# A mixer and expert block on one core: first adaLN pieces on TensorE in column strips, blocks 0 and 3 tile by tile, down chunks in column halves

## The reference

```python
u = modulate(rms_norm(x, norm_mix_g), sh_a, sc_a)      # h * (1 + scale) + shift
x = x + gt_a * mixer(u, w_in, ...)                     # mLSTM and dilated attention on one projection
u = modulate(rms_norm(x, norm_ffn_g), sh_f, sc_f)
x = x + gt_f * moe(u, router_w, ...)                   # 16 experts, group-limited top-2
return rms_norm(x, final_norm_g)
```

## Time and profile before

| | us |
|---|---|
| median of 3 runs | 624.14 |
| lowest, highest | 622.63, 625.4 |
| the profiled execution, whole | 625.4 |
| its span, first to last instruction | 623.5 |
| TensorE busy in the span | 579.7 (93%) |
| VectorE, ScalarE, GpSimd busy | 316.7, 229.3, 5.7 |

### The profile page before, as it was taken

One profiled execution on the slowest core, in us unless ns is written; L12 is line 12 of the kernel. 1 busy time (PEld: TensorE's weight loads), 2 busy tenths in 40 slices (PEclk: granted clock), 3 DMA queues, 4 the chain that ended last, 5 costly groups with the idle time before them and its releaser, 6 DMA issues.

```text
span 623.5 us, 8315 instructions
## 1 busy us (share of the span) xinstructions
PE 579.7 (93%) x3522; PEld 428.6 (69%) x3522; DVE 316.7 (51%) x467; ACT 229.3 (37%) x312; POOL 5.7 (1%) x14
## 2 busy tenths in 40 slices
PE   1599999999999999999999999989999999999784
PEld 0499988999998888999999885534543533533232
DVE  3797976767569786786464754312202122220203
ACT  4425748444555365376543434201201111110103
POOL 3000000000000000000000000000000000000000
PEclk9799999999999999999999998999999999999997
DMA  8996553785857944744599897399999999999981
GB/s 316 362 387 227 203 203 130 276 290 219 300 216 284 399 155 162 270 139 165 174 387 357 320 383 268 114 398 389 399 387 400 387 402 387 402 387 401 387 350 69
DMA packets 80584, 184.77 MB, mean 296 GB/s; under 512 B 5561, under 2 KB 5665, under 8 KB 78497
## 3 DMA queue, kind: packets, MB, share of 16 engines
q1 hardware_dynamic: 78018, 184.06, 79.6%
q10 hardware_dynamic: 2528, 0.16, 0.3%
HBM read 183.16 MB, written 1.05 MB: 295 GB/s over the span
## 4 chain that ended last, share of the span: by engine, by line
PE 82%; DMA 9%; DVE 4%; ACT 2%; SPq 2%; issue 1%; DVEq 0%; ACTq 0%
PE ps L1357 29%; PE ps L1365 15%; PE ps L1568 15%; PE ps L1580 7%; DMA ring<-in_w_down_e_dram 3%; DMA ring<-in_w_gate_e_dram 2%; DMA ring<-in_w_up_e_dram 2%; DMA raw<-in_w_in_dram 2%; PE ps L1604 2%; PE ps L1556 2%; PE ps L1345 1%; SPq L444 1%; PE ps L1523 1%; PE ps L1434 1%; PE ps L1470 1%
## 5 line engine op out<-in xcount | busy, mean ns | idle before, releaser
L803 DVE TENSOR_TENSOR lo<-raw,hi 128x2048 fp32r<-128x2048 f32 x52 | 118.8, 2291 | 43.3 <-ACT hi L539 43.0
L1357 PE MATMUL ps<-u_hi,hi 128*128 128x256 f32 x432 | 124.4, 288 | 1.1 <-DVE u_lo L869 1.1
L1357 PE MATMUL ps<-u_lo,hi 128*128 128x256 f32 x432 | 122.2, 283 | 0.0
L1357 PE MATMUL ps<-u_hi,lo 128*128 128x256 f32 x432 | 122.2, 283 | 0.0
L1568 PE MATMUL ps<-ring,xe_t 128*64 128x512 f32 x512 | 113.8, 594 | 7.6 <-DMA ring<-in_w_up_e_dram 3.9
L539 ACT CAST hi<-raw 128x2048 fp32r<-128x2048 f32 x52 | 98.7, 1906 | 51.4 <-PE ps L1357 24.6
L1568 PEld LDWEIGHTS ps<-ring,xe_t 128*64 128x64 f32 x512 | 37.5, 137 | 75.3 <-issue 75.2
L1357 PEld LDWEIGHTS ps<-u_hi,hi 128*128 128x128 f32 x432 | 82.8, 192 | 1.5 <-DVE u_lo L869 1.3
L1357 PEld LDWEIGHTS ps<-u_lo,hi 128*128 128x128 f32 x432 | 82.8, 192 | 0.2
L1357 PEld LDWEIGHTS ps<-u_hi,lo 128*128 128x128 f32 x432 | 82.8, 192 | 0.0
L1580 PE MATMUL ps<-ring,he_t 128*64 128x512 f32 x256 | 57.1, 596 | 1.5 <-DMA ring<-in_w_down_e_dram 0.7
(11 more groups left out here) (297 smaller groups left out, 803.3 us busy)
## 6 DMA issues: line engine op xcount, KB each, us to landing
raw<-in_w_in_dram SPq DMA_DIRECT2D x42, 1024.0 KB, 5.0
ring<-in_w_gate_e_dram SPq DMA_DIRECT2D x32, 1024.0 KB, 14.6
ring<-in_w_up_e_dram SPq DMA_DIRECT2D x32, 1024.0 KB, 14.2
ring<-in_w_down_e_dram SPq DMA_DIRECT2D x32, 1024.0 KB, 14.4
raw<-in_ada_w_dram SPq DMA_DIRECT2D x16, 1024.0 KB, 5.0
first_ada<-in_ada_w_dram SPq DMA_DIRECT2D x16, 512.0 KB, 11.6
raw<-in_w_branch_m_dram SPq DMA_DIRECT2D x4, 1024.0 KB, 7.2
raw<-in_w_out_dram SPq DMA_DIRECT2D x4, 1024.0 KB, 6.3
```

What stands on the lines that cost most here:

```text
L803: V.tensor_tensor(lo[b % RING][:], src[:], hi[b % RING][:].bitcast(F32), ALU.subtract).then_inc(lo_ready, 1)
L1357: ins = mm(dst, w[:, k, cols], x[:, k0 + k, :], start=(first and c % 2 == 0 and k == 0 and n == 0), stop=(end and k == KB - 1 and n == 2), ...
```

## The change

- **adaLN pieces.** Pieces 0 to 3 and 7 are multiplied by c on TensorE: four calls a piece, each with c's column broadcast to 32 columns as weights, each into its own 32 partitions of a PSUM bank (`row_sums`). VectorE copies the four rows of sums (`rows_out`), and four matmuls with a 0/1 matrix `pick_m` add the strips and turn them into columns. VectorE still sums pieces 4, 5 and 6 (semaphore `acc_done`), and two matmuls with ones add that sum to the strips of piece 7.
- **Order.** The plain matmuls ahead of the transposes are gone; pieces 0 and 1 stand there. A matmul in piece 2 to 3 and four behind the columns write a bank that nobody reads. In `FIRST` block 2 comes before piece 5. Block 3's load waits for `acc_done` 2, since piece 5 lies in its buffer.
- **Blocks 0 and 3** are rounded, split and multiplied tile by tile; block 0 is loaded in four DMAs.
- **Small loads.** The four small DMAs of ScalarE are issued by GpSimd after `chan1`.
- **ScalarE** loads the root's table ahead of the squares, and ahead of the last rounding of y at the end.
- **Down of the last pair.** Its four chunks are regrouped by columns: two hold columns 0 to 511 of both experts, whole contraction; the others, loaded in halves, columns 512 to 1023. `gate_y` and the splitting run by half, and four matmuls that nobody reads follow the first half's scatter.
- **Last norm.** Squares go half 0 first; VectorE multiplies half 0 by the gain early and ScalarE scales it, VectorE does half 1.

```diff
-FIRST = ([("ada", a) for a in range(4)] + [("w", 0), ("w", 1), ("ada", 4), ("ada", 5), ("w", 2), ("ada", 6), ("ada", 7),
+FIRST = ([("ada", a) for a in range(4)] + [("w", 0), ("w", 1), ("ada", 4), ("w", 2), ("ada", 5), ("ada", 6), ("ada", 7),
...
             for kind, n in FIRST:
-                if kind == "w":
+                if kind == "w" and n == 0:
+                    for k in range(KB):
+                        sp.dma_start(raw[0][:, k:k + 1, :], block_source((kind, 0))[:, k:k + 1, :]
+                                     ).then_inc(first_w[k] if k < KB - 1 else raw_loaded[0], 16)
+                elif kind == "w":
+                    if n == EARLY:
+                        sp.wait_ge(acc_done, 2)
...
-            for n in range(RSLOTS, CHUNKS):
+            for n in range(RSLOTS, CHUNKS - 4):
...
+            for q in range(2):
+                for e in range(2):
+                    n = CHUNKS - 2 + e
+                    sp.wait_ge(chunk_used, n - RSLOTS + 1)
+                    load_columns(n % RSLOTS, e, 1, (q,), last_loaded[e] if q else ring_loaded[n % RSLOTS])
...
+            after(pool, "chan1")
+            pool.dma_start(w_if[:], A["w_in"][0].rearrange("(k p) n -> p k n", p=P)[:, :, IF_AT:IF_AT + IF_N]).then_inc(small_loaded, 16)
+            pool.dma_start(gate_b[:], A["mlstm_gate_b"][0:1, :].broadcast_to([P, IF_N])).then_inc(small_loaded, 16)
+            pool.dma_start(rw[:], A["router_w"].rearrange("(k p) n -> p k n", p=P)).then_inc(small_loaded, 16)
+            pool.dma_start(rb[:], A["router_b"].rearrange("(a n) -> a n", a=1).broadcast_to([P, NE])).then_inc(small_loaded, 16)
...
+            act.wait_ge(consts_ready, 2)
+            A_(st[:, 36:37], ident[:, 0:1], ACT.Sqrt)
...
-            split_hi(0)
             after(act, "x_t")
...
+            def split_first(j):
+
+                hi_tile(j, 0)
+                hi_tile(j, 1)
+                u_hi_tile(j, 0)
+                u_hi_tile(j, 1)
+                hi_tile(j, 2)
+                u_hi_tile(j, 2)
+                hi_tile(j, 3)
+                u_hi_tile(j, 3)
...
+            def last_norm():
+
+                for n in range(2 * TT):
+                    if n:
+                        act.wait_ge(squared, n)
+                    last_square(n % TT, n // TT)
+                    if n >= TT:
+                        t = n - TT
+                        act.wait_ge(last_var, t + 1)
+                        A_(st[:, 32 + t:33 + t], st[:, 20 + t:21 + t], ACT.Sqrt).then_inc(last_sqrt, 1)
+                for t in range(TT):
+                    act.wait_ge(last_rms, t + 1)
+                    A_(result[:, t, 0:NB], result[:, t, 0:NB], ACT.Copy, scale=st[:, 34 + t:35 + t]).then_inc(out_act, 1)
...
+            def first_half(j, row_bank, col_bank):
+
+                rows_out(j, row_bank)
+                lo_tile(j, 0)
+                modulate(j, col_bank)
                 for k in range(KB):
-                    after(dve, f"u_hi0_{k}")
-                    event(V.tensor_tensor(u_lo[:, k, :], u_f32[:, k, :], u_hi[:, k, :].bitcast(F32), ALU.subtract), f"u_lo0_{k}")
...
+                    if k:
+                        lo_tile(j, k)
+                    u_tile(j, k)
...
+            first_half(0, 2, 3)
             split_lo(1)
             ada(4)
-            ada(5)
...
                 if s == 0:
+                    ada(5)
                     ada(6)
-                    ada(7)
-                    split_lo(EARLY)
-                    modulate(1, 7)
-                if s == 1:
-                    u_split_lo(1)
+                    first_half(1, 6, 7)
...
             for h in range(2):
+                dve.wait_ge(chunk_used, CHUNKS - 2 + 2 * h)
+                gate_y((h,))
                 dve.wait_ge(y_hi_ready, 2 * PAIRS - 1 + h)
                 split_y(h)
...
+            def row_sums(j, bank, a, start, stop):
+
+                pe.wait_ge(ada_landed[a], 32)
+                for i in range(2):
+                    for m in range(2):
+                        part, kk = 32 * (2 * i + m), 2 * (a % KB) + i
+                        ins = mm(ps[bank][part:part + 32, :], cs[:, kk:kk + 1].broadcast_to([P, 32]), first_ada[a][:, i, m, :],
+                                 start=start, stop=stop, skip_group_check=True)
+                ins.then_inc(rows_summed, 1)
+
             def mod_columns(j, bank):
 
-                pe.wait_ge(ada_done, 4 * (j + 1))
...
+                for c in range(KB):
+                    if c % 2 == 0:
+                        after(pe, f"row{j}_{c // 2}")
+                    ins = mm(ps[bank][:, 2 * c:2 * c + 2], ada_rows[:, j, c * P:(c + 1) * P], pick_m[:], start=True, stop=True,
+                             skip_group_check=True)
                 event(ins, f"mod_col{j}")
...
+            after(pe, "c_silu")
+            for a in range(2):
+                row_sums(0, 2, a, a == 0, False)
             after(pe, "x_norm")
-            for n in range(2):
-                mm(ps[2 + n][:], ident[:], x_in[:, 0, 0:NB], start=True, stop=True)
...
-            mod_columns(0, 1)
+            for a in (2, 3):
+                row_sums(0, 2, a, False, a == 3)
+                if a == 2:
+                    mm(ps[1][:], ident[:], first_ada[0][:, 0, 0, :], start=True, stop=True)
+            pe.wait_ge(pick_ready, 4)
+            mod_columns(0, 3)
+            for n in range(4):
+                mm(ps[1][:, 0:T], ident[:], first_ada[0][:, 0, 0, 0:T], start=True, stop=True)
...
-                        if s == EARLY - 1 and c == 2:
+                        if s == EARLY - 1 and c == 3:
                             after(pe, "x_up")
-                            mod_columns(1, 7)
+                            row_sums(1, 6, KT - 1, True, False)
+                            pe.wait_ge(acc_done, KB - 1)
+                            for m in range(2):
+                                ins = mm(ps[6][32 * m:32 * m + 32, :], ones[:, 0:32], acc_a[:, m, :], start=False, stop=True,
+                                         skip_group_check=True)
+                            ins.then_inc(rows_summed, 1)
...
+                            if s == EARLY - 1 and c == 3 and k == 2:
+                                mod_columns(1, 7)
...
+                    last_down(0, range(KB), group_slots(p * NPART + 4))
+                    slots = group_slots(p * NPART + 5)
+                    last_down(1, (0, 1), slots)
+                    for e in range(2):
+                        pe.wait_ge(last_loaded[e], 16)
+                    last_down(1, (2, 3), slots)
...
+                if h == 0:
+                    for _ in range(4):
+                        mm(ps[4][:], scat[1][:, 0:P], y_hi_e[:, 0:NB], start=True, stop=True)
```

More of the change, by code:

```diff
@@ L219, in build @@
         cs = small("cs", [P, KT])
+        pick_m = small("pick_m", [P, 2])
         st = small("st", [P, 40])
@@ L843, in _, with rows_out, lo_tile @@
             after(dve, "c_silu")
+            def rows_out(j, bank):
+                dve.wait_ge(rows_summed, (4, 6)[j])
+                for n in range(2):
+                    cols = slice(n * T, (n + 1) * T)
+                    event(V.tensor_copy(ada_rows[:, j, cols], ps[bank][:, cols]), f"row{j}_{n}")
+            def lo_tile(j, k):
+                b = EARLY * j
+                after(dve, f"hi{b}_{k}")
+                event(V.tensor_tensor(lo[b % RING][:, k, :], raw[POS[("w", b)] % RAW][:, k, :], hi[b % RING][:, k, :].bitcast(F32),
+                                      ALU.subtract), f"lo{b}_{k}")
             def modulate(j, bank):
@@ L1186, in fill_xe, with gate_y @@
                 ins.then_inc(xe_dve, 1)
-            def gate_y():
-                for h in range(2):
+            def gate_y(halves=(0, 1)):
+                for h in halves:
                     ins = V.tensor_tensor(y_e[:, h * NB:(h + 1) * NB], ps[6 + h][:], mod[:, 3, h * NB:(h + 1) * NB], ALU.mult)
@@ L1583, in down, with last_down @@
                                 ins.then_inc(chunk_used, 1)
+            def last_down(h, kk_of, slots):
+                for kk in kk_of:
+                    for s in range(2):
+                        w = ring[slots[s]][:].rearrange("p (k n) -> p k n", k=KB)
+                        ins = mm(ps[6 + h][64 * s:64 * s + 64, :], he_t[:, kk, s * SLOTS:(s + 1) * SLOTS], w[:, kk, :],
+                                 start=(kk == 0), stop=(kk == KB - 1))
+                        if kk == KB - 1:
+                            ins.then_inc(chunk_used, 1)
             def turn_slots(col, weights):
```

213 lines of the change are left out of this document (112 added, 101 removed).

## The result

The changed kernel took 618.0 us (median of ten runs, 617.07 to 621.85), the kernel before 624.31 beside it (ten runs, 622.52 to 626.61): ratio 0.9909, 95% interval 0.9884 to 0.9933.

A forecast was written before the change was run, and what follows sets the result against it. TensorE was taken to bound most of the span, with the expert stage bound by transfers whose start hangs on TensorE. Head 5.3 plus tail 1.9 made 7.2 us off the 624.1 median: 616.9 us, range 614.5 to 621.0.

The forecast's parts named there:

- Head, forecast 5.3: Start of the kernel up to block 4: block 4 starts at 50.75 instead of 56.0 us, 5.3 us earlier.
- Piece 1.05 and 1.9: adaLN pieces on TensorE: four strips side by side take 1.05 us a piece at full clock, 1.9 at half.
- Block 0 at 22.8 to 23.4: Start of block 0's matmuls: 22.8 to 23.4 us instead of 27.37.
- chan1 at 43.5, tile 0 at 44.4: Ahead of block 3: second scale and shift columns ready at 43.5 us, first tile of u at 44.4, starting block 3.
- 0.6 + 0.35 + 0.36 = 1.3 us: Within block 0: VectorE's time per tile, 1.3 us, below TensorE's 1.44, so TensorE leads if the clock stays up.
- Tail, forecast 1.9: End of the kernel, from the down halves to the last store: 1.9 us saved, with ends 0.8 and 3.
- the scatter's 0.43 us against 0.23: Last scatter on TensorE: each matmul takes 0.23 us instead of 0.43 if the clock stays up.
- A: Head: strips run only in pairs, head gain 2.4 us, total 619.8 us; chance 0.10.
- D: Head: strips run one after another, block 3 comes 5.8 us later, total 628.0 us; chance 0.05.
- B: Head: half clock lasts into block 0, which starts at about 25.5 us; head gain 2.5, total 619.7; chance 0.15.
- C: Before the experts: VectorE or a load swallows the head's gain, only the tail's stays, 622.2 us; chance 0.08.
- under 1 us for eight changes: Head: draining TensorE at eight changes of tiling mode costs under 1 us, and the sum stays.

The follow-up runs named there:

- both edits: The changed kernel without the filler matmul ahead of the fourth piece and with unused matmuls that hold the clock in the gaps: 616.66 us, ratio 0.9881.

## Why the prediction was right, point by point

**The size.** Forecast 7.2 us, medians 6.3, lower levels (617.83 against about 622.5) 4.7, profiled pair 8.6. That the medians agree with the sum is in part luck. Like with like, at the lower levels, the change is worth 4.7 us, 3.7 by the head and 1.0 by the end, against 5.3 and 1.9 forecast. The other 1.6 us come from the levels: the median run of the kernel before is one in which the clock had fallen more (624.3 against 622.5), that of the changed kernel is not. The forecast had no term for it. Nor had it one for the time outside the span: it took 1.9 us for both kernels, and the changed one has 0.3 more than the kernel before.

**Head, forecast 5.3, measured 4.7 by the profiled pair and 3.7 by the lower levels.** The mechanism stands, and in the profiled pair nearly every step. Piece 1.05 and 1.9: 1.06 and 1.93. Transposes end 17.2: 16.5. Third piece until 18.2: 17.5. Fourth until 20.1: 19.6. Columns 21.7: 21.24. Block 0 at 22.8 to 23.4: 22.98. split_lo(1) ends 29.2: 29.3. Issue of block 3's load 36.2: 36.22. The step that was mis-sized is "chan1 at 43.5, tile 0 at 44.4": chan1 was ready at 43.7, and the first tile of u took 1.3 us, since rounding (0.58), a hand-over (0.28 idle on VectorE) and subtraction (0.42) stand in line; block 3 began at 44.97. From there to block 4 the forecast had 6.35 us and the trace 6.37. The same chain stands ahead of block 0: from the end of the transposes to block 0 the forecast had 5.6 us and the trace 6.5. The columns took 1.04 us instead of 0.7, and chan0 to block 0 took 1.3 instead of 0.7. Block 0 came out at 22.98 only because the transposes ended 0.7 earlier than forecast, and that moment varies: other profiles with the same head have block 0 at 22.92, 23.48 and 23.75, and block 4 at 51.28, 51.82 and 52.10, 4.7 to 3.9 us ahead of 56.02. In the other profiles with the old head block 3 began at 49.76 to 50.13, up to 0.5 ahead of 50.26. So the pair first compared shows nearly the largest head gain of all.

**VectorE's part.** "0.6 + 0.35 + 0.36 = 1.3 us" per tile was 1.39 (starts of lo at 22.84, 24.23 and 25.62), and TensorE's 1.44 still led it. Behind the tiles VectorE leads by 0.35 us: TensorE waits that long for the next split block, ahead of block 1 and of block 4.

**Tail, forecast 1.9, measured 1.0 by runs, and 1.4 of the 2.3 us of the profiled pair.** The steps fit: 18.1 us were forecast from the start of the last down matmuls to the end (603.5 to 621.6), 17.7 measured. What the forecast got wrong is whose merit that is. It set the scatter's 0.43 us against 0.23 as a gain of the change; the run with the head alone has 0.23 with the old end. So does the kernel before with its waits filled. And it had no term for a stall at a branch, 1.82 us long, which took the new end's whole gain in the profile of the kernel before with the new end.

**The term that was missing.** The clock between 374 and 385 us, 1.7 us of the profiled pair. The forecast treated the stretch from block 4 to the reload as fixed; it is fixed but for these 1.7 us, and up to 3.4 in other profiles.

**Rivals.** A and D (strips in pairs or in line): refuted by the 1.06 us piece and by the kernel with two strips. B (half clock into block 0): not seen in any profile with the new head; all ran 20 to 34 us at 1.00. On the ground that the forecast gave for it: sixteen transposes took 1.97 us, all at full pace, in the kernel with block 3's load freed, 2.63 in the changed kernel and 3.62 in the kernel with both edits, where only the strips behind them ran at full pace. The clock thus rose before, during and behind the transposes. The Trainium skill (TensorE: Matmul & The Clock Gate, Part 4) says that full clock does not engage for transposes, which it does not count as busy in the same way. The rows differ from that in one point: transposes did run at full pace, all sixteen of them in 1.97 us. In that kernel the pace had risen within piece 1 (1.82 us instead of 1.93), ahead of them. Whether transposes help the clock to rise no run shows. But B's mechanism did strike in another place: the clock fell before block 3 and at 374 us. C (gain swallowed): refuted by 4.71 us still there at 367 us.

**Switching between strips and full width.** In the changed kernel's order of time the transposes' last record ends at 13.88 + 2.63 = 16.51 and the third piece's first starts at 16.44. The drain that the Trainium skill names (TensorEngine Tiling (Array Packing), Key Properties) shows as no gap here. Since the ends of matmuls are modelled in the profile, that says only that it is short, as the forecast had put it (under 1 us for eight changes).

**What holds the two levels.** Of the seven kernels with the new head, four strips and no holding matmuls, 22 of 49 runs lay above 619.5 us; of the two with them, none of twelve. That the gaps set off the fall is shown by that and by the kernel before with only the later place filled. Why the clock falls in one run and not in the next stays open, since TensorE's work is the same in both. The Trainium skill (TensorE: Matmul & The Clock Gate, What's actually happening) says that how many matmuls pass before the clock rises differs between runs of one kernel; whether the falls here vary for the same reason no run shows.

## What to carry to other kernels

A multiplication of a vector by a wide matrix fits in a strip of 32 columns, and four strips beside each other cost TensorE what one full-width product does; that takes such sums off VectorE, where they delayed everything at the start here. When the time of a kernel has two levels, sort the runs by granted clock and look for half-pace stretches behind TensorE's short waits: matmuls into an unused bank that end before the wait does cost nothing there, while one that stands ahead of data already landed costs its full length. Before crediting an edit with a stretch that got shorter, look whether the clock of that stretch differs without the edit, and compare runs of like clock.

## What the runs showed that I had not expected

- TensorE's clock fell behind waits of 0.68 to 0.94 us (1.55 in one kernel) in some runs of a program and not in others; where the first sums met it, they took 5.38 to 6.71 us in place of 3.68. With these waits filled, none of 12 runs of the changed kernel lay on the upper level.
- A stall of 1.82 us with no releaser, at a place where the program branches, was 0.79 us in the one profile with 64 waits put in some 600 us earlier, and did not exist in another kernel with the same lines.
- TensorE's clock first rose within piece 1 in one profile and only behind the sixteen transposes in others; these took 1.97 to 3.68 us, and block 0 moved with them.
- The fourth small load on ScalarE's queue held that engine for 5.51 us; from GpSimd's queue the same four took 1.03, 0.56, 0.89 and 0.56 us to issue. With the small loads under way the core's loads ran at 350 GB/s instead of 387.
